# The second mixer of a two-model fp32 kernel with its heads, weight splits and PSUM banks in another order

## The reference, cut to what matters

```python
h = rms_norm_2(x, attn_norm)
proj = h @ w_in                       # 1024 x 5444
aq, ak, av, iq, ik, iw, bq, bk, bv, gates = split_cols(proj)
ya = sparse_attention(...)            # 8 heads, keys chosen by an index score of iq, ik, iw
yb = diff_attention(bq, bk, bv, lam)  # 4 differential heads, each of two softmaxes
yb = rms_norm_2(yb, b_subln) * (1.0 - lam_init)
g_a, g_b = jnp.split(jax.nn.sigmoid(gates + gate_bias), 2, axis=-1)
merged = g_a * (ya @ w_up_a) + g_b * (yb @ w_up_b)
x = x + merged @ w_out
```

## Time and profile before

| | |
|---|---|
| median of 3 runs | 1890.23 us (1889.31 to 1891.76) |
| profiled execution | 1888.97 us |
| its span, first to last instruction | 1887.3 us |
| TensorE busy | 1806.5 us, 96% of the span |
| VectorE, ScalarE, GpSimd busy | 1114.6, 928.5 and 188.5 us |
| granted TensorE clock over the span | 0.986 of full speed |

### The profile page before, as it was taken

The page is one execution under the profiler, slowest core; times in us unless marked ns, Lnnn a source line. Parts: engine busy times, 40 slices in busy tenths (PEclk is TensorE's granted clock), DMA queues, the critical chain, the costliest instruction groups (busy, mean ns, idle before and its releaser), DMA issues.

```text
span 1887.3 us, 23610 instructions
## 1 busy us (share of the span) xinstructions
PE 1806.5 (96%) x8739; PEld 1470.8 (78%) x8739; DVE 1114.6 (59%) x1647; ACT 928.5 (49%) x1259; POOL 188.5 (10%) x226
## 2 busy tenths in 40 slices
PE   6999999999999999999999887999999888999999
PEld 5888877788888888777888765788888766788887
DVE  5554676655455546776554576665544585675552
ACT  5443475544354435755443654545443645545441
POOL 0000020000000001100000383000001453000000
PEclk9999999999999999999999998999999989999999
DMA  7656462565555564625556443255555532365551
GB/s 233 192 178 214 144 184 90 164 193 178 207 172 179 179 226 136 186 83 177 180 178 225 157 156 107 98 190 187 178 178 192 201 122 79 134 201 179 178 196 71
DMA packets 221018, 316.21 MB, mean 168 GB/s; under 512 B 14057, under 2 KB 162177, under 8 KB 220673
## 3 DMA queue, kind: packets, MB, share of 16 engines
q1 hardware_dynamic: 220928, 315.03, 50.7%
HBM read 313.94 MB, written 1.05 MB: 167 GB/s over the span
## 4 chain that ended last, share of the span: by engine, by line
PE 83%; DVE 6%; issue 4%; ACT 2%; POOL 2%; DVEq 1%; DMA 1%; SPq 1%; POOLq 1%; ACTq 0%
PE ps L1740 25%; PE ps L1742 25%; PE ps L1741 25%; DVE w_lo L1086 2%; PE ps L1845 2%; ACT w_hi L651 1%; PE ps L1750 1%; PE ps L1933 1%; PE ps L1921 1%; PE ps L1909 1%; POOL rg L608 1%; PE ps L1878 1%; DVEq L1537 1%; ACT att L952 1%; PE ps L2213 0%
## 5 line engine op out<-in xcount | busy, mean ns | idle before, releaser
L1086 DVE TENSOR_TENSOR w_lo<-raw,w_hi 128x2048 fp32r<-128x2048 f32 (+1 forms) x298 | 674.9, 2286 | 276.8 <-ACT w_hi L651 275.5
L1740 PE MATMUL ps<-w_hi,aT_hi 128*128 128x512 f32 (+2 forms) x1760 | 706.3, 401 | 22.3 <-ACT proj L911 12.9
L1742 PE MATMUL ps<-w_hi,aT_lo 128*128 128x512 f32 (+2 forms) x1760 | 688.1, 391 | 0.0
L1741 PE MATMUL ps<-w_lo,aT_hi 128*128 128x512 f32 (+2 forms) x1760 | 686.9, 390 | 0.0
L651 ACT ACTIVATE w_hi<-raw 128x2048 fp32r<-128x2048 f32 (+1 forms) x298 | 556.4, 1900 | 181.9 <-PE ps L1742 170.3
L1740 PEld LDWEIGHTS ps<-w_hi,aT_hi 128*128 128x128 f32 x1760 | 335.1, 190 | 100.7 <-issue 35.5
L1742 PEld LDWEIGHTS ps<-w_hi,aT_lo 128*128 128x128 f32 x1760 | 334.4, 190 | 70.5
L1741 PEld LDWEIGHTS ps<-w_lo,aT_hi 128*128 128x128 f32 x1760 | 335.3, 191 | 62.2
L701 ACT ACTIVATE att<-ps,rstd 128x256 f32<-128x256 f32 x132 | 55.4, 471 | 377.9 <-PE ps L1742 377.8
L1160 DVE SCALAR_TENSOR_TENSOR att<-ps,rstd,att 128x256 f32<-128x256 f32 x132 | 57.8, 479 | 287.2 <-ACT att L701 287.2
L1740 PE MATMUL ps<-w_hi,gT_hi 128*128 128x512 f32 x528 | 207.1, 392 | 0.0
(11 more groups left out here) (252 smaller groups left out, 1333.3 us busy)
## 6 DMA issues: line engine op xcount, KB each, us to landing
raw<-in_w_in SPq DMA_DIRECT2D x120, 512.0 KB, 4.6
raw<-in_w_ffn_gate SPq DMA_DIRECT2D x88, 512.0 KB, 4.1
raw<-in_w_ffn_up SPq DMA_DIRECT2D x88, 512.0 KB, 5.2
raw<-in_w_ffn_down SPq DMA_DIRECT2D x88, 512.0 KB, 4.4
raw<-in_w_ffn_in SPq DMA_DIRECT2D x88, 512.0 KB, 4.9
raw<-in_w_ffn_out SPq DMA_DIRECT2D x44, 512.0 KB, 4.7
raw<-in_w_out SPq DMA_DIRECT2D x32, 512.0 KB, 4.6
raw<-in_w_ck SPq DMA_DIRECT2D x8, 512.0 KB, 4.1
```

The costliest lines, as they stand in the source:

```text
L1086: V.tensor_tensor(o, a, h, ALU.subtract).then_inc(units_split, 1)
L1740: M(o, ah, wh, start=start, stop=False)
L1741: M(o, ah, wl, start=False, stop=False)
L1742: return M(o, al, wh, start=False, stop=stop)
```

## The change

It rewrites the order of the second mixer on all queues. TensorE's head work sits at later and evenly spaced positions: each pair's `pair_turn` stands eleven positions behind its `pair_qk`. The tiles from 4 on rotate through banks 0, 1 and 3 instead of using 0 and 1 each time. The splits stand in the queues of ScalarE and VectorE where their slots fall free. The gate tiles are computed in the order 2, 3, 0, 1 (the differential gates first), and the up products of the differential heads come ahead of the sparse ones; their input is kept in new tensors `yb_hi` and `yb_lo`, which lie over old queries and keys. SP loads five tiles, not two, ahead of the bias. The work itself, its shapes and its counts stay, but for three table loads more on ScalarE in each layer (45 in the program in place of 39).

```diff
-       [(3396 + 512 * g, 512) for g in range(4)]
+       [(3396 + 512 * g, 512) for g in (2, 3, 0, 1)]
 IN1 = 2840
...
-        BANK2 = ((0, 1), (2, 3), (0, 1), (2, 3)) + ((0, 1), ) * 7
-        UP_BANKS = ((0, 1), (2, 3), (4, 5), (6, 7))
+        BANK2 = ((0, 1), (2, 3), (0, 1), (2, 3), (0, 1), (3, 0), (1, 3), (0, 1), (3, 0), (1, 3), (0, 1))
+        UP_BANKS = ((4, 5), (0, 1), (6, 7), (2, 3))
...
-                win_loads(st, l, P2_WIN, I["w_in_2"], WIN2[:2])
+                win_loads(st, l, P2_WIN, I["w_in_2"], WIN2[:5])
...
-                win_loads(st, l, P2_WIN + 4, I["w_in_2"], WIN2[2:])
+                win_loads(st, l, P2_WIN + 10, I["w_in_2"], WIN2[5:])
                 for u in range(4):
-                    p, w = P2_UP + u, I[("w_up_a_2", "w_up_b_2")[u % 2]]
+                    p, w = P2_UP + u, I[("w_up_b_2", "w_up_a_2")[u % 2]]
...
+                evac(0)
+                if l == 0:
+                    split(st, 3)
+                head_squares(0)
                 win_split(2, 0)
-                evac(0)
-                head_squares(0)
                 head_roots(0)
                 act.wait_ge(lam_sums, l + 1)
                 nc.scalar.activation(lam[:, 0:2], lam[:, 0:2], ACT.Exp).then_inc(lam_exp, 1)
                 win_split(2, 1)
+                if l == 0:
+                    for i in range(2):
+                        nc.scalar.activation(x[:, i, :], xn[:, i, :], ACT.Copy, scale=rstd[:, 2 + i:3 + i])\
+                            .then_inc(x_ready, 1)
+                    nc.scalar.drain()
                 win_split(3, 0)
...
-                item(4)
                 win_split(5, 1)
                 head_roots(3)
+                item(4)
+                win_split(6, 0)
                 exps(0)
-                win_split(6, 0)
+                evac(4)
+                win_split(6, 1)
+                probs_turned(0)
+                split(st, P2_WIN + 14)
                 exps(1)
-                evac(4)
-                probs_turned(0)
-                win_split(6, 1)
                 diff_out(0)
...
                 act.wait_ge(yb_ms, l + 1)
                 nc.scalar.activation(ms[:, 0:8], ms[:, 0:8], ACT.Sqrt).then_inc(yb_root, 1)
+                exps(6)
+                sparse_hi(0)
                 split(st, P2_UP)
+                act.wait_ge(tile_done, W + 9)
+                gate(GATES2 + DM)
+                probs_turned(6)
...
                 win_split(5, 0)
+                best(1)
                 head_sums(3)
+                win_split(5, 1)
+                head_scales(3)
+                best(1)
                 item(5)
                 best(1)
-                win_split(5, 1)
-                head_scales(3)
+                win_split(6, 0)
                 masked(0)
                 best(1)
-                win_split(6, 0)
                 probs(0)
+                win_split(6, 1)
                 masked(1)
                 best(1)
-                win_split(6, 1)
+                split(st, P2_WIN + 14)
                 probs(1)
...
+                gate(9, 0)
+                split(st, P2_UP)
+                probs(6)
+                sparse_lo(0)
+                gate(9, 1)
+                probs_turned(6)
+                masked(7)
+                split(st, P2_UP + 1)
                 probs(7)
...
                     def wait(i):
-                        if i == 1:
+                        used = [(m, j) for m in range(n) for j in range(2) if BANK2[m][j] == BANK2[n][i]]
+                        if not used:
+                            return
+                        m, j = used[-1]
+                        if j == 1:
                             pe.wait_ge(tile_done, W + m + 1)
...
+                def beside_ak(at):
+                    if at == 8:
+                        pair_turn(0)
+                    if at == 9:
                         pair_qk(1)
-                    if at == 15:
-                        pair_turn(0)
-
-                def beside_ak(at):
-                    if at == 4:
-                        pair_qk(2)
+                    if at == 12:
                         pe.wait_ge(tile_done, W + 5)
                         diff_pv(0)
...
+                    if at == 12:
+                        pair_turn(3)
+                    if at == 13:
                         copied(5, 5)
                         pair_qk(4)
 
                 def beside_g1(at):
                     if at == 0:
+                        diff_pv(3)
+                    if at == 8:
+                        pair_turn(4)
+                    if at == 9:
                         pair_qk(5)
...
                 def beside_g3(at):
                     if at == 0:
+                        pair_turn(6)
+                    if at == 1:
+                        pair_qk(7)
+                    if at == 4:
                         sparse_pv(6)
+                    if at == 8:
+                        pe.wait_ge(yb_ready, l + 1)
+                        pe.wait_ge(pair_T_act, J + 7)
+                        pe.wait_ge(pair_T_dve, l * 4 + (PAIRS1 * L + 3))
+                        for i in range(2):
+                            turned(xn, i, 1, STAGE_BANKS_YB)
+                    if at == 12:
                         pair_turn(7)
...
+                up(0, yb_hi, yb_lo, 0, diff_ready, beside_b0)
+                up(1, ya_hi, ya_lo, 0, sparse_ready, lambda at: None)
+                up(2, yb_hi, yb_lo, 0, lambda i, c: None, beside_b1)
+                up(3, ya_hi, ya_lo, 0, lambda i, c: None, lambda at: None)
```

More of the change, by code:

```diff
@@ L895, in _ @@
                     root(N, 4)
-                    split(st, 3)
-                    for i in range(2):
-                        nc.scalar.activation(x[:, i, :], xn[:, i, :], ACT.Copy, scale=rstd[:, 2 + i:3 + i])\
-                            .then_inc(x_ready, 1)
                 else:
@@ L1020, in _ @@
-                probs_turned(1)
-                split(st, P2_WIN + 14)
-                exps(3)
-                diff_out(1)
                 evac(5)
                 head_squares(4)
+                split(st, P2_WIN + 15)
+                item(6)
+                probs_turned(1)
+                head_roots(4)
+                exps(2)
+                diff_out(1)
+                split(st, P2_WIN + 16)
+                evac(6)
                 probs_turned(2)
-                split(st, P2_WIN + 15)
@@ L1669, in _ @@
                 V.drain()
+                masked(3)
+                split(st, P2_WIN + 17)
                 item(9)
-                masked(4)
+                probs(3)
+                split(st, P2_WIN + 18)
                 dve.wait_ge(bias_loaded, (l + 1) * 16)
@@ L1719, in _ @@
                 split(st, P2_OUT + 2)
+                up_a(1, 0)
+                up_a(1, 1)
                 stage(B + 6, parts=((0, 1), (1, 1)), first=2, banks=STAGE_BANKS_UP)
```

266 lines of the change are left out of this document (128 added, 138 removed).

## The result

| | before | after |
|---|---|---|
| median | 1890.97 us (1889.31 to 1891.76, 4 runs) | 1848.01 us (1846.75 to 1848.92, 4 runs) |
| profiled execution | 1888.97 us | 1847.19 us |
| span | 1887.3 us | 1845.5 us |
| granted clock over the span | 0.986 | 0.999 |

A forecast was written before the change was run, and what follows sets the result against it. TensorE, busy 96%, bounds the kernel. Of 67.5 us to win, 8.9 and 5.4 of waits, 3.2 of side jobs and 1.7 of half clock come off: 48.3 net, 1840.7 profiled, 1842 us median; range 1826 to 1859.

The forecast's parts named there:

- 67.5: Both second mixers: all there is to win, 48.7 us of TensorE waits plus 18.8 us lost to half clock.
- half clock: TensorE at the 1.2 GHz level after waits: one stretch of 3.4 us after the longest remaining wait, costing 1.7 us.
- `item(1)`: First layer's mixer: a near miss at this item, 0.5 us given back.
- pair 0's scores and tile 5's bank: TensorE waits for tile 4's evacuation behind pair 0's exponentials: 4.1 us in the first layer, 1.9 in the second.
- VectorE's stretch up to pair 0: VectorE from tile 4's first split to pair 0's first operation: no idle time to close up, 30.6 us.
- The signs named: First turn without wait, mixers 23 to 27 us shorter; wrong if GpSimd's later passes cause waits or half clock exceeds 7.
- All pairs but two come out with 1 to 2 us of slack: Heads' probabilities: the 17.0 us of waits go; only pairs 3 and 6 wait, 0.6 and 1.6 us a layer.
- the second layer's first rotations: TensorE's first turn there: GpSimd's rotations have next to no slack, 0.4 us given back.
- (a): Rival: no wait worth naming is left, TensorE reaching each place later than counted; 63 us won, 1827 us; chance 0.08.
- (b): Rival: remaining waits are larger and each throws the clock down; 20 to 25 us less won, 1862 to 1867; chance 0.19.
- (c): Rival: slower; VectorE splits stretch GpSimd's eight-head passes beyond 24.3 us, the last late; 1904 us at 26; chance 0.04.
- (d): Rival: no change within 0.2%; waits return at tile 5's bank and the probabilities, needing 24 us a mixer; chance 0.03.

The follow-up runs named there:

- two banks: The changed kernel with banks 0 and 1 alone for all tiles from 4 on: 1859.46 us.
- norm later: The changed kernel with GpSimd's pass over the differential heads' output held back until pair 4's probabilities are done: 1846.55 us.
- bank first: The changed kernel with ScalarE's evacuation of tile 4 ahead of pair 0's exponentials: 1845.85 us.
- both: The changed kernel with tile 4's evacuation ahead of pair 0's exponentials, turns of pairs 2, 4, 6 two positions later, item 8's copy ahead of pair 3's exponentials: 1837.84 us.
- pair 0 first: The changed kernel with later turns, earlier item 8 copy, and VectorE's pair 0 masked scores and probabilities ahead of tile 6's split and a key-choice round: 1843.68 us.

## Why the prediction was right, and which steps were not

**The sum.** I take the 67.5 as won, as counted. Given back: waits of 11.0 us in the first layer (8.9 predicted) and 10.6 in the second (5.4), half clock 1.7 (1.7), and what is left of the span's 41.8, 67.5 - 21.6 - 1.7 - 41.8 = 2.4, for the side jobs (3.2). Of the 7.3 us of waits too few, 5.2 are the second layer's. By place, pairs 2 and 4 are 5.7 us, the rotations 3.1 and `item(1)` 0.9; the other terms together came out 2.4 smaller than counted.

| term | predicted, layers 1 and 2 | measured |
|---|---|---|
| tile 1's second unit | 1.2, none | 1.30, none |
| `item(1)` | 0.5, none | 1.43, none |
| rotations: later ones in layer 1, the first in layer 2 | none, 0.4 | 0.79 + 0.28, 2.40 |
| pair 0's scores and tile 5's bank | 4.1, 1.9 | 0.59 + 1.88, 0.30 + 2.77 |
| `pair_turn(3)` | 0.6, 0.6 | 0.35, 0.72 |
| `pair_turn(6)` | 1.6, 1.6 | 1.00, 1.00 |
| `pair_turn(2)`, `pair_turn(4)` | none | 1.44 + 1.41, 1.44 + 1.41 |
| `up_a(1, 0)` | 0.9, 0.9 | 0.56, 0.56 |

**Right.** The place and the order of the gain (the start, the banks, the spacing, each by undoing it: 9.9, 11.4 and, for two of its eleven positions, 19.3 us); VectorE's stretch up to pair 0 (30.6, measured 31.10); pair 0 near 1121 (1121.86); the single stretch at half clock, behind the longest wait, at the bank of tile 5; no wait at any other bank; differential gates first at no cost that shows. The single stretch is in part luck: another wait, of 2.40 us, stayed without one, and in some of the other kernels it did not.

**The signs named** did not all come. The first turn waited 2.40 us in the second layer, the mixers are 21.9 and 20.5 us shorter and not 23 to 27, and waits for GpSimd's later passes show in the first layer (0.79 and 0.28 us), which stood among the signs of being wrong. VectorE's stretch and the half clock (3.41 us) stayed within their bounds.

**The step that failed** is "All pairs but two come out with 1 to 2 us of slack". Slack of 1 us or more had pairs 5 (1.0) and 7 (4.3), and pair 0 in the second layer (3.1; 0.6 in the first); pair 1 came with none, pairs 2 and 4 missed by 1.4. I had worked out each chain with durations of operations that ran alone, 1.4 us for `probs`. Beside GpSimd it took 3.4 in pairs 0 and 1 of the first layer and 3.7 in pair 4. For pair 4 the cause is shown by the run that moved GpSimd's pass away. For pair 2 it is argued from the trace: in the 15 us ahead, L1588 (2.66), L1527 (1.20) and the split (3.36) together took 4.0 us more than alone (0.75, 0.22, 2.28); no run took that pass away by itself.

**Mis-sized** were the second layer's first rotations (0.4, measured 2.40) and `item(1)` (0.5, 1.43; on VectorE it stands behind L1527, 1.14 us beside GpSimd where 0.22 is its length alone, and a split). The first layer's bank was counted too high (4.1, measured 2.5 with pair 0's scores) and the second's too low (1.9, 3.1): waits ahead of it that I had not counted held TensorE back there, so that in the first layer it asked at 1123.6 and not at 1120.5. That hid part of the error. For the rotations the trace gives a reason. GpSimd's first pass has small operations of 0.32 us, and each that meets a split of VectorE lasts as long as the split. The timeline of the kernel after, second layer:

```profile
1467.16 2.26 POOL L588 TENSOR_TENSOR proj<-proj,rg 128x64 f32<-128x64 f32 x1
1469.39 2.37 POOL L589 TENSOR_TENSOR proj<-proj,rg 128x64 f32<-128x64 f32 x1
1471.89 0.33 POOL L594 TENSOR_TENSOR proj<-proj,rg 128x64 f32<-128x64 f32 x1
```

Four were hit in that pass, three in the run with late loads, where the turn waited 0.63 instead of 2.40.

**The rivals.** (a) did not come about. (b) in its first half did: larger waits than counted, but they did not throw down the clock each, and the time stayed well under 1862. (c)'s threshold was never near: GpSimd's first three passes of eight heads took 15.4, 14.2 and 13.9 us in the first layer against 24.3. But its mechanism is what made the forecast too good, on the other engine: not GpSimd's long passes, VectorE's short operations were late. (d) was far off; its 24 us are 3.4 times the 7.2 that my sum has for a mean layer, not five times.

**The spacing** was half understood. Two positions less at every pair cost 19.3 us, and three turns two positions later won 5.5. But in that last run pairs 3, 5 and 7 had nine positions, and nothing was lost there. So the distance from the scores is not by itself the limit. What counts is when VectorE, in its own order, comes to the pair's probabilities: pair 3's stand behind `item(9)`, as predicted, and its wait is the same 0.4 and 0.7 us for scores two positions later. For the other pairs this reading is argued from the order, not shown.

## What to carry to other kernels

Evacuate first what a slow engine is waiting for, and place TensorE's small jobs by the time at which the engine that feeds them gets there in its own queue, with contention, not by a fixed distance: where two engines' work can overlap, take each short operation of the one at the length of the other's, and ask where it will fall. Put single edits together when each takes a wait of its own away; here two measured alone (2.2 and 5.5) and one read from a trace (2.1) added up to 10.2, while one that reordered VectorE instead put the probabilities of pairs 0 and 1 wholly in GpSimd's way and ended 5.8 above.

## What the runs showed of the hardware

**VectorE and GpSimd stretch one another by whole operations.** A scaling by `probs` of 0.28 to 0.35 us took 1.08 to 1.35 beside GpSimd operations of about that length; a VectorE operation on 16 columns 1.20 in place of 0.22 (L1527 in the kernel after); a GpSimd one of 0.32 took 2.26 and 2.37 beside splits of 2.3. The price is what is left of the neighbour, so a short operation pays most, but a long one pays too: the split at 1143.56 started 0.07 us behind a GpSimd operation of 1.29 and took 3.36 in place of 2.28. Not every operation is hit. `masked`, which reads PSUM and one operand in SBUF, kept its length beside GpSimd's L595, in the run with pair 0 first:

```profile
1120.14 1.29 POOL L595 TENSOR_TENSOR proj<-proj,rg 128x512 f32<-128x512 f32 x1
1120.16 0.29 DVE L1566 CUSTOM_DVE_ANT_0 att<-ps,causal 128x128 f32<-128x128 f32 x1 [0.23 <-issue]
...
1120.38 0.42 DVE L1566 CUSTOM_DVE_ANT_0 att<-ps,causal 128x256 f32<-128x256 f32 x1
```

The Trainium skill (SBUF — State Buffer, "Who interferes with whom") says the same: a VectorE instruction with at most one SBUF input, outside the two-port modes, doesn't contend with GpSimd. These rows agree, 0.29 and 0.42 us; the same two operations of pair 1 in the kernel after, from 1131.24 on with GpSimd idle, take 0.29 and 0.42 as well.

**The same wait, with and without half clock.** The second layer's first turn waited 2.40 us in the kernel after and TensorE's clock stayed at full speed; in the run with tile 4's evacuation first it waited 2.43, and a stretch of 3.41 us at half clock lay over it. Nine profiles have this wait, at 2.38 to 2.43 us. In four (two banks, norm later, bank first, both) such a stretch begins within 1.3 us of the turn, and pair 0's scores then wait 1.2 to 1.4 us; in the other five there is none, and they wait 0.3. So that loss comes and goes with the clock and not with the edits; why, no run shows. And the first layer's twelve waits of 0.3 to 1.9 us in the kernel after had no stretch at all, where four fell into the same mixer before, each at a wait of 2.4 us or more. But length alone does not decide: the wait of 1.88 at the first layer's bank had a stretch behind it in the run with the late start. What decides stays open here.
